# Three modulation gates move out of an input projection, to the places just ahead of two later stages

## The reference, cut to what matters

```python
mod = (silu(cond) @ w_ada[i] + b_ada[i]).reshape(cond.shape[0], 6, 1, 1024)
sh1, sc1, ga1, sh2, sc2, ga2 = (mod[:, t] for t in range(6))
hn = rmsnorm(x, g_norm1[i]) * (1.0 + sc1) + sh1
out = mixer_i(hn)                       # mLSTM (i = 0) or RWKV (i = 1)
x = x + ga1 * out
hn = rmsnorm(x, g_norm2[i]) * (1.0 + sc2) + sh2
ff = swiglu(hn) if i == 0 else moe_swiglu(hn)   # the router's logits are hn @ w_router
x = x + ga2 * ff
```

## Time and profile before

| | us |
|---|---|
| median of three timed runs | 2788.75 |
| the profiled execution, its own time | 2785.02 |
| its span, first to last instruction | 2782.9 |
| PE busy in the span | 2565.0 |
| DVE busy | 1173.5 |
| ACT busy | 563.3 |
| mean granted PE clock | 0.971 of full |

### The profile page before, as it was taken

How to read it: one execution, slowest core, us unless ns; L and a number is a source line. 1 busy time by engine, 2 the same in 40 slices (tenths; PEclk the granted TensorE clock), 3 DMA queues, 4 the chain that set the end, 5 groups by cost and what they waited for, 6 DMA issues and landing times.

```text
span 2782.9 us, 64247 instructions
## 1 busy us (share of the span) xinstructions
PE 2565.0 (92%) x29049; PEld 2077.2 (75%) x29049; DVE 1173.5 (42%) x2067; ACT 563.3 (20%) x975; POOL 265.1 (10%) x166
## 2 busy tenths in 40 slices
PE   5999879999999979978888888889899999999995
PEld 3666556677776757747777777776799999999995
DVE  4534677544463376646655555537200000000004
ACT  3101222100000010024544444431210111011002
POOL 0000240000000000003333322210100000000001
PEclk9999999999999989979999999999999999999997
DMA  7663112321222022310000000002455555655553
GB/s 318 274 242 151 46 46 78 142 68 69 76 78 83 36 74 105 126 42 4 23 23 23 23 23 23 6 20 93 147 209 206 187 202 213 214 183 202 206 209 128
DMA packets 56525, 321.39 MB, mean 115 GB/s; under 512 B 8096, under 2 KB 15520, under 8 KB 25568
## 3 DMA queue, kind: packets, MB, share of 16 engines
q1 hardware_dynamic: 46016, 281.32, 28.1%
q10 hardware_dynamic: 6816, 19.66, 2.0%
q0 software_dynamic: 3456, 16.78, 1.5%
HBM read 288.38 MB, written 29.36 MB: 114 GB/s over the span
## 4 chain that ended last, share of the span: by engine, by line
PE 85%; DVE 7%; ACT 3%; issue 3%; DMA 1%; SPq 0%; ACTq 0%; POOL 0%; DVEq 0%; POOLq 0%
PE PS L883 35%; PE PS L1528 17%; PE PS L1543 8%; PE PS L1138 3%; PE PS L1271 3%; PE PS L1263 2%; PE PS L861 2%; PE PS L1203 1%; PE PS L1253 1%; PE PS L1335 1%; DMA arena<-in_k 1%; PE PS L603 1%; PE PS L1196 1%; ACT arena L1820 1%; PE PS L978 1%
## 5 line engine op out<-in xcount | busy, mean ns | idle before, releaser
L883 PE MATMUL PS<-arena,ring 128*128 128x320 f32 x2680 | 748.7, 437 | 25.1 <-DVE arena L2441 12.3
L883 PEld LDWEIGHTS PS<-arena,ring 128*128 128x128 f32 x2680 | 511.0, 192 | 250.7 <-issue 23.8
L1528 PE MATMUL PS<-arena,ring 128*128 128x192 f32 x2816 | 471.0, 331 | 7.5 <-issue 4.4
L1528 PEld LDWEIGHTS PS<-arena,ring 128*128 128x128 f32 x2816 | 468.5, 194 | 8.9 <-issue 4.8
L1543 PE MATMUL PS<-arena,ring 128*128 128x192 f32 x1408 | 230.1, 326 | 0.0
L1543 PEld LDWEIGHTS PS<-arena,ring 128*128 128x128 f32 x1408 | 229.0, 190 | 0.0
L2708 DVE TENSOR_TENSOR arena<-arena,PS 128x192 f32<-128x192 f32 x88 | 31.2, 354 | 448.5 <-ACT arena L1942 448.5
L883 PE MATMUL PS<-arena 128*128 128x320 f32 x536 | 151.1, 432 | 0.0
L883 PEld LDWEIGHTS PS<-arena 128*128 128x128 f32 x536 | 101.8, 190 | 42.4
L802 POOL TENSOR_TENSOR arena<-arena,const 128x512 f32<-128x512 f32 (+1 forms) x24 | 26.7, 1115 | 1095.4 <-DVE arena L2542 764.6
L1271 PE MATMUL PS<-arena 64*64 64x64 f32 x3200 | 119.0, 220 | 9.5 <-issue 9.1
(11 more groups left out here) (343 smaller groups left out, 3167.7 us busy)
## 6 DMA issues: line engine op xcount, KB each, us to landing
ring<-in_k SPq DMA_DIRECT2D x145, 1024.0 KB, 4.9
arena<-in_k SPq DMA_DIRECT2D x48, 1024.0 KB, 9.3
ring<-in_exd SPq DMA_DIRECT2D x32, 1408.0 KB, 6.0
ring<-in_ffd SPq DMA_DIRECT2D x8, 1408.0 KB, 6.2
rkv_s<-arena ACTq DMA_DIRECT2D x24, 320.0 KB, 4.1
expert_rows<-arena POOLq DMA_DIRECT2D x4, 1536.0 KB, 10.3
x<-in_x SPq DMA_DIRECT2D x2, 2560.0 KB, 9.1
expert_rows<-arena ACTq DMA_DIRECT2D x8, 512.0 KB, 3.8
```

What stands on the lines that cost most here:

```text
L883: m = pe.matmul(out, lhs[:, k], rhs[:, k], start=k == 0, stop=k == count - 1)
L1528: m = pe.matmul(PS[:, k % 4, t * CAP:(t + 1) * CAP], w[:, kt, t * P:(t + 1) * P], xe[:, kt], start=kt == 0, stop=kt == KT - 1)
```

## The change

The groups are put in a new order (`GROUPS`): nine *early* ones, and three *late* ones, the groups 5, 8 and 11, which get the numbers 9, 10 and 11. `k8` is laid out in that order. The early ones run ahead of and between the input projection's slabs as before, the last behind slab 7. The late ones have memory places and PSUM banks of their own:

- Late 9 and 10 are loaded by SP behind the first three slabs of the mLSTM's output projection and `C_out`. PE does group 9 ahead of `norm(1)`, group 10 behind it, once ACT has made the root (`norm_std`). ACT copies both behind `norm_b(1)`; PE turns both behind slab 1 of the feed-forward, DVE adds the bias behind slab 2.
- Late 11 is loaded behind slab 2 of the RWKV output projection (the fourth load, slab 3, follows it). PE does it between `norm(3)` and the router's logits, ACT copies it behind `norm_b(3)`, PE turns it ahead of the gather of the first expert's tokens, DVE adds the bias behind `place`.
- The fourth slab of the mLSTM's output projection now stands behind `C_out` and behind late 9 and 10 in SP's queue, and the credit `states_out` stands ahead of late 10.
- POOL's clearing of the expert rows waits until PE has used late 9 and 10.

```diff
+EARLY = (0, 1, 2, 3, 4, 6, 7, 9, 10)
+LATE = (5, 8, 11)
+GROUPS = EARLY + LATE
...
+        late_at = {9: (25472, 27520, 29568, 31616), 10: (10240, 12288, 14336, 23040), 11: (12288, 14336, 16384, 18432)}
+        SPLIT_KT, split_at = 5, 33664
...
+        late_rows = {9: hid_f[:, FT - 2, 0:256], 10: hid_f[:, FT - 1, 0:256]}
+        late_bank = {9: PS[:, 7, 256:512], 10: PS[:, 6, 0:256], 11: PS[:, 5, 0:256]}
+        late_turned = {9: PS[:, 7, 0:256], 10: PS[:, 6, 256:512], 11: PS[:, 0, 256:512]}
...
-            return None if k % 6 == 5 or k >= 12 else 2 + k // 6 * 5 + k % 6
+            return None if k % 6 == 5 or k >= 8 else 2 + k // 6 * 5 + k % 6
...
+            def late_load(g):
+                for q in range(ADA_SLOTS):
+                    a, whole = late_at[g][q], (g, q) != (10, 3)
+                    n = W8 if whole else SPLIT_KT * 256
+                    sp.dma_start(arena[:, a:a + n], k8[4 * g + q][:, 0:n]).then_inc(ada_slab_ready[q], 16)
+                    if not whole:
+                        sp.dma_start(arena[:, split_at:split_at + W8 - n], k8[4 * g + q][:, n:]).then_inc(ada_slab_ready[q], 16)
...
-            stream(sp, k8, 61, 4, W8)
+            stream(sp, k8, 61, 3, W8)
             mdve.wait(sp, f"C{NU - 1}")
             sp.dma_start(A["C_out"], Cst[:, :, 1, :]).then_inc(out_done, 16)
+            mdve.wait(sp, "hn9")
+            late_load(9)
             sp.wait_ge(out_done, 48)
             credit(sp, states_out, 1)
+            late_load(10)
+            stream(sp, k8, 64, 1, W8)
             stream(sp, k8, 65, 22, W8)
...
-            stream(sp, k8, 102, 3, W8)
+            stream(sp, k8, 102, 2, W8)
+            late_load(11)
+            stream(sp, k8, 104, 1, W8)
...
-            pool.wait_ge(ada_used, 12)
+            pool.wait_ge(ada_used, len(EARLY))
...
             pool.wait_ge(norm_std, 2)
+            pool.wait_ge(ada_used, 11)
             pool.memset(zeros, 0.0).then_inc(zeroed, 1)
...
+            def late_group(group):
+                for q in range(4):
+                    pe.wait_ge(ada_slab_ready[q], 16 * (group + (q == 3 and group > 9)))
+                for kt in range(KT):
+                    for q in range(4):
+                        m = pe.matmul(late_bank[group][32 * q:32 * q + 32], scond[:, kt, :], late_tile(group, q, kt), start=kt == 0, stop=kt == KT - 1)
+                m.then_inc(ada_used, 1)
...
             slab_n["pe"] += 4
+            late_group(9)
             norm(1)
+            pe.wait_ge(norm_std, 2)
+            late_group(10)
...
+                if k == 1:
+                    late_columns(9)
+                    late_columns(10)
             slab_n["pe"] += FT
...
             norm(3)
             ro_dve.wait(pe, "m2", 3)
+            late_group(11)
             pe.wait_ge(wrouter_in, 16)
...
             m.then_inc(logits_full, 1)
+            pe.wait_ge(ada_copied, len(GROUPS))
             for n in range(1, 5):
                 token_major(n)
...
             pe.wait_ge(placed, 1)
+            late_columns(11)
...
+            pe.wait_ge(ada_done, len(GROUPS))
             pe.wait_ge(routes_ready, 1)
...
             norm_b(1, hn_f, 0, 1)
+            copy_late(9)
+            copy_late(10)
...
             norm_b(3, hn2, 1, 1)
+            copy_late(11)
...
+                if k == 2:
+                    ada_columns(9)
+                    ada_columns(10)
+                    dve.wait_ge(ada_done, 11)
...
             i.then_inc(placed, 1)
+            ada_columns(11)
+            dve.wait_ge(ada_done, 12)
             dve.wait_ge(exp_done, 1)
```

More of the change, by code:

```diff
@@ L317, in build, with late_tile @@
         ada_slab1 = [slab_of(z[:, 13:26].rearrange("p a b -> p (a b)"), k) for k in range(ADA_SLOTS)]
+        late_at = {9: (25472, 27520, 29568, 31616), 10: (10240, 12288, 14336, 23040), 11: (12288, 14336, 16384, 18432)}
+        SPLIT_KT, split_at = 5, 33664
+        def late_tile(group, q, kt):
+            at = late_at[group][q] + kt * 256
+            if group == 10 and q == 3 and kt >= SPLIT_KT:
+                at = split_at + (kt - SPLIT_KT) * 256
+            return arena[:, at:at + 256]
         ada_rows = ada_region[:, ADA_SLOTS * KT * 256:][:, 0:2 * 256].rearrange("p (g n) -> p g n", g=2)
@@ L426, in build @@
         sge = r(4, CAP)
+        late_rows[11] = sge.rearrange("p a b -> p (a b)")[:, 0:256]
         slots, place, where0 = r(CAP), r(CH, CAP), r(CH)
@@ L637, in _ @@
                 g = ada_after(k)
-                if g and g + 1 < 12:
+                if g and g + 1 < len(EARLY):
                     sp.wait_ge(ada_used, g + 1)
@@ L869, in ada_columns, with late_columns @@
                 m.then_inc(ada_t, 1)
+            def late_group(group):
[5 more added lines that the diff above has]
+                m.then_inc(ada_used, 1)
+            def late_columns(group):
+                pe.wait_ge(ada_copied, group + 1)
+                for h in range(2):
+                    m = pe.transpose(late_turned[group][:, h * P:(h + 1) * P], late_rows[group][:, h * P:(h + 1) * P], cst("ident"))
+                m.then_inc(ada_t, 1)
             ada_group(0, 0)
@@ L934, in _ @@
                     ada_group(g, 6)
-            pe.wait_ge(ada_done, 11)
-            ada_columns(11, 7)
+            pe.wait_ge(ada_done, len(EARLY) - 1)
+            ada_columns(len(EARLY) - 1, 7)
             slab_n["pe"] += 48 + 13
@@ L941, in _ @@
             pe.wait_ge(in_fin, 4)
-            pe.wait_ge(ada_done, 12)
+            pe.wait_ge(ada_done, len(EARLY))
             mact.wait(pe, "dec")
@@ L1623, in _, with copy_late @@
             copy_rows(1, 1)
+            def copy_late(group):
+                act.wait_ge(ada_used, group + 1)
+                act.activation(late_rows[group], late_bank[group], ACT.Copy).then_inc(ada_copied, 1)
             def norm_b(n, buf, layer, which):
@@ L2117, in _, with ada_columns @@
             mf = mods[:].rearrange("p l k t s -> p (l k t) s")
-            def ada_columns(group, bank):
+            def ada_columns(group, bank=None):
                 dve.wait_ge(ada_t, group + 1)
-                src = PS[:, bank, 0:256].rearrange("p (h q r) -> p q h r", h=2, q=4)[:, :, :, 0:2]
+                src = (late_turned[group] if bank is None else PS[:, bank, 0:256]).rearrange("p (h q r) -> p q h r", h=2, q=4)[:, :, :, 0:2]
                 b0 = VEC["b_ada"][0]
-                out = mf[:, bass.ds(group * 8, 8), :].rearrange("p (q h) s -> p q h s", h=2)
-                b = vec[:, bass.ds(group * 8 + b0, 8)].rearrange("p (q h) -> p q h", h=2).unsqueeze(3).to_broadcast([P, 4, 2, 2])
+                out = mf[:, bass.ds(GROUPS[group] * 8, 8), :].rearrange("p (q h) s -> p q h s", h=2)
+                b = vec[:, bass.ds(GROUPS[group] * 8 + b0, 8)].rearrange("p (q h) -> p q h", h=2).unsqueeze(3).to_broadcast([P, 4, 2, 2])
                 dve.tensor_tensor(out, src, b, ALU.add).then_inc(ada_done, 1)
@@ L2826, in layout @@
     eg = a["w_exp_gu"][0].reshape(NE, D, 2, ET, P).transpose(0, 1, 3, 2, 4).reshape(NE, D, 2 * ET * P)
-    out["k8"] = np.concatenate([slab8(a["w_ada"][0]), slab8(a["w_ada"][1]), slab8(wi), slab8(a["w_m_out"][0]), slab8(gu),
+    ada = np.concatenate([slab8(a["w_ada"][0]), slab8(a["w_ada"][1])])
+    out["k8"] = np.concatenate([ada[4 * np.array(GROUPS)[:, None] + np.arange(4)].reshape(48, P, KT * 256), slab8(wi), slab8(a["w_m_out"][0]), slab8(gu),
                                 slab8(rkv), slab8(lo), slab8(a["w_rwkv_out"][0])] + [slab8(eg[e]) for e in range(NE)])
```

## The result

The changed kernel takes 2761.76 us (median of four runs, 2759.33 to 2766.58) where the kernel before takes 2789.24: a ratio of 0.991, with a 95% interval of 0.9887 to 0.9934. So about 12 us were forecast, and 17 to 27 came. The profiled execution of the changed kernel took 2766.58 us, its span is 2764.8, which is 18.1 us shorter than the span before.

The account below looks back on a forecast made before the run. PE bounds the kernel, busy 92% of the span; moved work costs little in its gaps. -11.73 + 0.7 + 0 + 0.62 - 1.7 + 0.31 = -11.8 us from 2788.75 gives 2777.0 us, range 2768 to 2786.

Parts of the forecast that it names:

- Removed: Input projection: three groups with their transposes leave, 3.91 us each, 11.73 us saved.
- Group 9 and 10: Around norm(1): group 9 ahead adds 0.7 us; group 10 behind costs 0, hidden by ACT's scale and shift.
- Transposes of the two: Feed-forward, behind slab 1: two pairs of transposes on PE's path, 0.62 us added.
- Logits: Between norm(3) and the logits: group 11 fills PE's 3.83 us gap, keeping the clock up, 1.7 us gained.
- Transposes ahead of the gather: Behind the logits: one pair of transposes ahead of the gather adds 0.31 us on PE.
- The forecast from clock to logits: Router's logits: with the gap filled, they run at clock 1.00 and take under 9 us.
- The covers: Rival: gaps filled by groups 10 and 11 run at half clock; sum -7.9 us, 2780.9 us; chance 0.20.
- moved at their full price: Rival: groups cost at the new places what they cost at the old; nothing gained, 2788.8 us; chance 0.10.
- the late loads: Rival: they get ahead of the mLSTM output projection's weights, slab 0 17.1 us late, 2794.1 us; chance 0.04.
- The step that failed: Unpriced assumption, no term in the sum: stages the change doesn't touch keep their time.
- the last clause of what would prove it wrong: Sign against the forecast: time lost in stages that the change doesn't touch; no size given.
- The first expert's products: Sign for the forecast: the first expert's products start 12 us earlier.

Follow-up runs that it names:

- the two traces: Profiles of the unaltered changed kernel from its first measurement (2761.76 us, 0.991) and its repeat with more rounds (2766.2 us, 0.994).
- ahead of a slab: Changed kernel with group 11 ahead of the RWKV output projection's last slab instead of the logits, result in PSUM bank 7: 2777.48 us, 0.9963 of the kernel before.
- the second measurement: The changed kernel, unaltered, timed again with more rounds beside the kernel before: 2766.2 us against 2783.36, ratio 0.994 (0.9925 to 0.9956).
- five profiles with the old counts: Kernel before, its repeat (0.9999), it with 64 tiny matmuls (0.9998), groups 5 and 8 alone late (0.9988), changed kernel with 34 tiny matmuls (0.9953).
- the pair alone: Against the kernel before, only groups 5 and 8 moved late, group 11 left in the input projection: 2781.61 us, 0.9988 (0.9975 to 1.0002).

## Why the prediction came out too high

**What held.** Each term of the sum is in the trace. *Removed:* -12.36 us at the last transposes, where -11.73 had been forecast; 0.33 of it stood there at the first slab already. At the mLSTM's first products -11.06 are left, since the clock fell behind the projection (0.50 from 274 to 277 us; twelve records there take 2.82 us instead of 1.53). *Group 9 and 10:* +0.78 and +0.77 us in the two traces, from the output projection's last four chains (454.77 against 465.61) to the second half of the feed-forward's first slab (481.60 against 491.66), where 0.7 and 0 had been forecast. *Transposes of the two:* +0.44, where 0.62 had been. *Logits:* -1.65 and -1.69 from the norm's second half to their end, where -1.7 had been. *Transposes ahead of the gather:* nothing that can be seen (-0.25 and -0.01 us between logits and gather), where +0.31 had been. These measured terms, from -11.06 and -11.04 on, add up to -11.7 and -11.5 us, the forecast to -11.8. The forecast from clock to logits held as well: the logits at 1.00, in under 9 us. The Trainium skill ("TensorE: Matmul & The Clock Gate", Part 1: The HAM clock gate) has activity release the low clock; the group that began at 0.50 and ended near 1.00, with the logits behind it at 1.00, agrees.

**What fell of the rivals.** The covers did not run at half clock but for the first microsecond of group 11. The groups were not moved at their full price: in the gap ahead of the logits 5.0 us less than ahead of a slab. And the late loads came ahead of nothing: the output projection's first chains start 10.48 us earlier than before (393.23 against 403.71 in the earlier trace rows), and at the second half of the feed-forward's first slab the changed kernel was still 10.06 us ahead.

**The step that failed** is one that the sum took without a term: that a stage which the change doesn't touch keeps its time. It stands only as the last clause of what would prove it wrong, and there as time lost. Instead the RWKV mixer's last stretches gained some 5 us, because 136 records of PE left the program ahead of them and the gaps that come every 256 records fell on other instructions. (The first expert's products, which were to start 12 us earlier, start 20.6 and 15.9 us earlier in the two traces; the low clock at the end of RWKV, below, is in both numbers.) That the counts are the cause, and no effect of filled gaps (B), is shown by the kernel before with 30 useless matmuls, which fills no gap and gains the same 5.9 us there, by 64 of them, which gain nothing, and by the changed kernel with 34 of them, which loses it. The page of before had a sign of it, since the earlier trace rows carries 3% "issue" in the chain, some 80 us, of which 21 us are 29 gaps of over 0.3 us at these counts, all in the RWKV mixer; the prediction read none of it as something that the change could move. The 3.98 us of "issue" in front of the first expert stand at another count.

**What stays open.** -11.8 and -5 make -17, which is the second measurement. The low clock at the end of RWKV (3.3 us) was absent from all profiles with the changed counts and from two of the five with the old ones; whether a gap in front of it sets it off, or chance does, these profiles don't tell: the gap of 1.4 us in the one line stands ahead of it in all five profiles with the old counts, and the clock fell behind it in three. The first measurement's 27 us lie 8 us further still, on four executions; the two intervals overlap from 0.9925 to 0.9934. Whether the pair alone gains its terms was not resolved either: 3.3 us were measured and its trace has 5.0, but its interval reaches to 7.0. No version was found that beats the changed kernel.

## What to carry to other kernels

Price moved work as here: whole duration where the engine never waits, nothing where it fills a gap that another engine sets, and look at the clock behind the gap. But this long unrolled program has a second clockwork: removing or moving some hundred instructions ahead of a stage of short ones shifted where its instruction stream is held up, and that alone was worth 0.2%, nearly half of the edit's own terms. Before a small gain is put down to an edit, pad the program so that the counts stay the same, and measure both.

## What the hardware showed that was not expected

PE stood still every 256 records of its own list where the records were short: in 45 us with 1484 records, ten gaps of 0.4 to 1.5 us, 8.2 us in all. The transfer table of a stretch there (queue, kind: packets, MB, share of the engines' time), before, from 1815 to 1860:

```profile
q8 instruction: 12, 0.20, 1.9%
```

That is one packet of 16384 bytes for each 256 records of 64 bytes. The packet that goes with a gap starts only behind it, but the one before ends 1.2 to 1.6 us ahead of the gap's end each time, so by the times PE stands there for its next block of instructions. Where a matmul takes 0.44 us, as in the slabs of the input projection, the timelines show no such gaps. The Trainium skill ("Runtime: NRT & Kernel Launch", Instruction fetch mechanics) says that instructions come in blocks of 16 KiB, 256 instructions, and that crossing such a boundary is mostly hidden. The size agrees with the trace; hidden it is not in this stage, where it takes 18% of the time (8.2 of 45.0 us).

The same gaps cost 5 us more or less by what they hit, and adding 30 matmuls that nobody reads made the kernel 0.2% faster. The clock of PE fell in stages that were the same code in the same place: 3.3 us at the end of RWKV, some 8 us in the mLSTM behind 16 added matmuls.
